# Prompt attention of a decoder step: split fp32r products against plain fp32 in halves of TensorE's array

## The chip, the cores and the metric

The kernel runs on one core of one Trainium2 chip. The metric is the device time of one execution in microseconds, the median of several. The engines are named as the profile names them: PE is TensorE (PEld its weight loads), DVE is VectorE, ACT is ScalarE, POOL is GpSimd, SP is SyncE, whose queue issues DMAs.

## The reference, cut to what matters

One layer of a decoder is computed for a prompt of 1024 tokens and for a sample group of 8 x 8 tokens. The change touches only the attention of the prompt. It has 8 heads of stick-breaking attention and 8 heads of dilated attention, all of width 64.

```python
def _sb_attend(q, k, v, mask, sb_bias):            # kind SB, strictly causal
    z = jnp.einsum('bqhd,bkhd->bhqk', q, k) * (q.shape[-1] ** -0.5) + sb_bias[...]
    log_1m = jnp.where(mask, jax.nn.log_sigmoid(-z), 0.0)
    excl = lax.cumsum(log_1m, axis=3, reverse=True) - log_1m
    a = jnp.where(mask, jnp.exp(jax.nn.log_sigmoid(z) + excl), 0.0)
    return jnp.einsum('bhqk,bkhd->bqhd', a, v)

def _dilated_prompt(q, k, v, rel_bias):            # kind DIL, three dilations, one softmax over all
    for window, dil in ((128, 1), (512, 4), (2048, 16)):
        ...
        logits = where(valid, q.k * scale + bias(distance), -inf)
        lse = logsumexp(logits); p = exp(logits - lse); o = p @ v
    return sum of the o's weighted by softmax of the lse's
```

The three dilations together are one softmax over all earlier keys, whose bias depends on the distance alone and holds the logarithm of how many dilations reach that key. The kernel computes it so, from a table `by_distance`.

## The kernel before, in words

The kernel is a row of stages, one after the other: transposing the tokens, the input projection, a stage that writes keys and values in their natural layout, the attention of the prompt (`prompt_stage`), the attention of the sample group, the output projection, the MLP, and the final norm. A stage ends with a barrier of all engines, so no work of one runs beside another's.

`prompt_stage` walks over four pairs of heads (`j`), and in each over 32 units: 16 of kind SB, then 16 of kind DIL. A unit `t` is one head and one tile of 128 queries against all keys up to it, so it is 128 to 1024 columns wide; the widths go up for the first head of the pair and down for the second. All five engines run the same walk, each a few steps later than the one before it, and wait for each other through counting semaphores:

- Step 0, TensorE `score`: queries times keys. To reach fp32 accuracy with the one-pass type fp32r, each operand is split into a rounded high part and the rest. `q_both` holds the high part of 64 rows and the low part in the other 64 rows, so one product with `k_hi` and one with `k_lo` give all four parts over 128 rows (line 958). For kind SB a bf16 product adds the causal mask (line 962). There are two score buffers of 1024 columns.
- Kind SB: ScalarE `gate` makes the sigmoids `take` and `stay` (lines 1035, 1037); VectorE `broken` makes the running product of `stay` from the right with a scan (line 1117) and multiplies it into `take` (line 1121).
- Kind DIL: VectorE `dilated` adds the bias (line 1134) and takes the maximum (1142) and its negative (1144); ScalarE `exponent` makes the exponentials with their sum (1043); VectorE `invert` inverts the sum (1149); ScalarE `soften` scales the weights by it (1048).
- Step 2, TensorE `turn`: transposes of the weights, in blocks of 128 columns, into one PSUM tile of 1024 columns (line 972). ScalarE `turned_hi` copies them out rounded (1054), and VectorE `turned_lo` writes the rest (1155). The next unit's transposes wait for line 1155.
- Step 3, TensorE `values`: 256 columns at a time (high and low weights) against high and low values as the 128 columns of the other operand (line 983). The two halves of the result are added: ScalarE copies the left half (1063), VectorE adds the right one (1165).
- Eight times in a pair and kind, `fold_heads` brings both heads' outputs to the right rows with two plain fp32 products against a constant matrix (line 992), and ScalarE copies them out (1069).

GpSimd splits queries, keys and values (lines 892 to 910) for each head and kind, while the units of the former head run, and issues the store of the outputs. SP's queue loads one head at a time, twice into both halves of the rows. What sets the order is this written walk: each engine's queue is in order.

Plain fp32 products stand elsewhere in the program: sums over rows with `ones` (line 486), and the scores and values of the sample stage (lines 1428 and 1499). In program order a unit of the sample stage has 16 products at line 1428, each on 32 columns of the array; the trace shows 32 records for them, two for each product. At line 1499 it has 32 products on 16 columns each, and 64 records.

Of the kernel before, what the change touches and what calls it, by code (L numbers as in the profile page):

```python
# [727 lines left out]
def prompt_stage(nc, cx, qkvT, oT, by_distance, sb_bias, neg_causal, ident, fold, v_nat):  # L728

# [18 lines left out]
    NU = 4 * QT  # L748
    HU = 2 * QT
    WS = 4  # L750


    FW = SEQ // 4
    fold_with = {**{1 + c: (DIL, c) for c in range(4)}, **{HU + 1 + c: (SB, c) for c in range(4)}}


    units = [(u // HU, (u % QT, QT - 1 - u % QT)[u // QT % 2], u // QT % 2) for u in range(NU)]
    with ExitStack() as st:
# [3 lines left out]
        q_raw, k_raw = sb("q_raw", [P, SEQ]), sb("k_raw", [P, SEQ])  # L762
        v_raw = sb("v_raw", [P, QT, HD])
        q_both = sb("q_both", [P, 2, SEQ], F32R)
        k_hi = sb("k_hi", [P, 2, SEQ], F32R)
        k_lo = sb("k_lo", [P, 2, SEQ], F32R)
        v_both = sb("v_both", [P, 2, QT, 2, HD], F32R)
        bias = sb("bias", [P, HEADS, SEQ])
        stay = sb("stay", [P, 2, SEQ])
        take = sb("take", [P, WS, SEQ])  # L770
        prod = sb("prod", [P, SEQ + 1])
        wtsT = sb("wtsT", [P, 2, QT, 2, P], F32R)
        o_sum = sb("o_sum", [P, 2, 2, SEQ])
        o_left = sb("o_left", [P, 2, P])
        o_T = sb("o_T", [P, SEQ])
        folds = sb("folds", [P, 2, P])
        top = sb("top", [P, 2, 2])
        den = sb("den", [P, HU])
        inv = sb("inv", [P, HU])
# [4 lines left out]
        s_ps = st.enter_context(nc.psum_tensor("pr_scores", [P, 2, 2 * 512], F32))  # L784
        t_ps = st.enter_context(nc.psum_tensor("pr_turned", [P, SEQ], F32))
# [5 lines left out]
        tables_in, tables_ready, bias_in = sem("tables_in"), sem("tables_ready"), sem("bias_in")  # L791
        q_loaded, v_loaded, k_loaded = sem("q_loaded"), sem("v_loaded"), sem("k_loaded")
        q_hi_done, q_done, k_hi_done, qk_ready = sem("q_hi_done"), sem("q_done"), sem("k_hi_done"), sem("qk_ready")
        v_hi_done, v_ready = sem("v_hi_done"), sem("v_ready")
        scored, sb_gates, sb_scanned, sb_weights = sem("scored"), sem("sb_gates"), sem("sb_scanned"), sem("sb_weights")
        logits, topped, lowered, exped, inverted, dil_weights = (sem("logits"), sem("topped"), sem("lowered"),
                                                                 sem("exped"), sem("inverted"), sem("dil_weights"))
        turned, hi_out, turned_out, o_done, o_summed = (sem("turned"), sem("hi_out"), sem("turned_out"), sem("o_done"),
                                                        sem("o_summed"))
        left_out, folded, oT_free, oT_stored = sem("left_out"), sem("folded"), sem("oT_free"), sem("oT_stored")  # L800

        def pipeline(eng, step, late):

            for s in range(NU):
                step(0, None, s)
            with eng.Fori(1, PAIRS) as j:
                for s in range(NU):
                    step(j, j - 1, s)
            for s in range(late):
                step(None, PAIRS - 1, s)  # L810

        def unit(j, prev, t):

            return (j, t) if t >= 0 else (prev, t + NU)

        def no_former(j):
            return isinstance(j, int) and j == 0

        def width(t):
            return (units[t][1] + 1) * P  # L820

        with nc.Block() as block:
            @block.sync
            def _(sp):
                def load(j, x):
                    kind, h = x // 2, x % 2
                    rows = [j * P + (g * W + h * HD) for g in (3 * kind, 3 * kind + 1)]
                    rows = rows if isinstance(j, int) else [sp.snap(a) for a in rows]
                    head = j * 2 + h if isinstance(j, int) else sp.snap(j * 2 + h)

                    sp.wait_ge(q_done, j * 4 + (x + 1))
                    for half in range(2):
                        sp.dma_start(q_raw[half * HD:(half + 1) * HD, :], qkvT[ds(rows[0], HD), 0:SEQ]).then_inc(q_loaded, 16)

                    sp.wait_ge(qk_ready, j * 4 + (x + 1))
                    for half in range(2):
                        sp.dma_start(k_raw[half * HD:(half + 1) * HD, :], qkvT[ds(rows[1], HD), 0:SEQ]).then_inc(k_loaded, 16)

                    sp.wait_ge(v_ready, j * 4 + (x + 1))
                    sp.dma_start(v_raw[:, :, :], v_nat[kind][0, 0].rearrange("(t p) h d -> p t h d", p=P)[  # L840
                        :, :, ds(head, 1), :].rearrange("p t o d -> p t (o d)")).then_inc(v_loaded, 16)

                for x in range(4):
                    load(0, x)
                    if x == 0:
                        sp.dma_start(zb[:, 0, :], bass.AP(
                            sb_bias.tensor, sb_bias.offset, [[0, P], [1, HEADS]])).then_inc(tables_in, 16)
                        sp.dma_start(maskf[:, :], neg_causal).then_inc(tables_in, 16)
                        sp.dma_start(folds[:, :, :], fold).then_inc(tables_in, 16)
                    if x == 1:  # L850
                        for h in range(HEADS):

                            first = by_distance.offset + h * LD + DIST0 - (SEQ - 1)
                            sp.dma_start(bias[:, h, :], bass.AP(by_distance.tensor, first,
                                                                [[1, P], [1, SEQ]])).then_inc(bias_in, 16)
                with sp.Fori(1, PAIRS) as j:
                    for x in range(4):
                        load(j, x)

            @block.gpsimd  # L860
            def _(pool):
                pool.sem_inc(q_done, 1)
                pool.sem_inc(v_ready, 1)
                pool.sem_inc(qk_ready, 1)
                pool.sem_inc(oT_free, 1)

                def split_first_v():

                    pool.wait_ge(v_loaded, 16)
                    pool.tensor_copy(v_both[:, 0, :, 0, :], v_raw[:, :, :]).then_inc(v_hi_done, 1)  # L870
                    pool.wait_ge(v_hi_done, 1)
                    pool.tensor_tensor(out=v_both[:, 0, :, 1, :], in0=v_raw[:, :, :],
                                       in1=v_both[:, 0, :, 0, :].bitcast(F32), op=ALU.subtract).then_inc(v_ready, 1)
                    pool.wait_ge(qk_ready, 2)
# [62 lines left out]
            def _(pe):  # L937
# [58 lines left out]
                def step(j, prev, s):  # L996
                    if j is not None:
                        score(j, s)
# [950 lines left out]
```

## Time and profile before

| | |
|---|---|
| time, median of 3 runs (lowest, highest) | 2310.68 us (2309.94, 2316.21) |
| the profiled execution's own time | 2313.0 us |
| its span, first to last instruction | 2311.1 us |
| mean granted TensorE clock over the span | 0.891 |
| PE busy | 1813.8 us (78%) |
| DVE busy | 1080.2 us (47%) |
| ACT busy | 631.1 us (27%) |
| POOL busy | 685.1 us (30%) |
| the stage of the prompt's attention | 403.5 to 870 us of the span |

Busy time is the union of an engine's instructions. It is an average over stages with different limits, so it has to be read stage by stage. The granted clock is a share of full speed: 1.00 is 2.4 GHz and 0.50 is 1.2 GHz, and a value between them is a mix of the two over a stretch. Matmul records overlap each other, because their printed ends include the way through the array; how fast they follow one another is read from several in a row.

### The profile page before, as it was taken

Reading aid. Unit: us, or ns where it says so; the run is one execution under the profiler, and the core shown is the slowest. Engines: PE = TensorE matmul, PEld = TensorE weight load, DVE = VectorE, ACT = ScalarE, POOL = GpSimd, SP = SyncE. Lnnn points to the kernel's source line nnn. Section 1 sums busy time; section 2 is a strip of 40 time slices with the busy share of each in tenths; the row PEclk is TensorE's granted clock in tenths of the full one; section 3 lists DMA queues with packets and bytes.
Section 4 is the critical chain, followed back from the end, with each engine's and each line's share of the span. In section 5 each row is a group of like instructions: output and inputs, shape, how many; then the busy total and the mean of one; then the engine's idle time right before and its main releaser. Section 6 shows DMA issues by size and latency. Waiting matters only on the chain. (4 is left out here: it accounts for less than half of the span.)

```text
span 2311.1 us, 37788 instructions
## 1 busy us (share of the span) xinstructions
PE 1813.8 (78%) x15810; PEld 1645.1 (71%) x15810; DVE 1080.2 (47%) x1229; ACT 631.1 (27%) x1068; POOL 685.1 (30%) x473
## 2 busy tenths in 40 slices
PE   4999995577666671565566639799999999999998
PEld 4999993456555550243334438789999999999997
DVE  5301112899897972876676445562222222122223
ACT  4100001476767670222032130131212112121122
POOL 2112101434343402566556631122112122121120
PEclk7999996787888885778887879899999999999999
DMA  6222218622222104999999970143433334333332
GB/s 210 76 85 103 85 48 317 167 55 55 56 56 65 45 10 135 411 419 423 421 421 420 406 300 1 37 164 109 146 127 127 139 114 144 128 127 131 122 109 104
DMA packets 129657, 382.35 MB, mean 165 GB/s; under 512 B 35416, under 2 KB 68824, under 8 KB 117464
## 3 DMA queue, kind: packets, MB, share of 16 engines
q0 software_dynamic: 41344, 256.13, 28.3%
q1 hardware_dynamic: 84840, 122.25, 16.5%
q10 hardware_dynamic: 3360, 2.47, 0.4%
q8 instruction: 70, 1.15, 0.2%
q14 instruction: 43, 0.35, 0.1%
HBM read 345.10 MB, written 102.57 MB: 194 GB/s over the span
## 5 line engine op out<-in xcount | busy, mean ns | idle before, releaser
L404 POOL TENSOR_TENSOR mlp_w_lo<-mlp_raw,mlp_w_hi 128x2048 fp32r<-128x2048 f32 x30 | 138.1, 4604 | 587.2 <-ACT mlp_w_hi L450 587.2
L1428 PE MATMUL sa_s<-sa_kT,sa_qd 128*32 128x256 f32 x1344 | 119.3, 516 | 156.7 <-DVE sa_kT L1692 96.3
L563 DVE TENSOR_TENSOR xT<-xT,mlp_acc 128x1088 f32<-128x1088 f32 x64 | 82.5, 1289 | 279.3 <-PE mlp_acc L145 279.3
L972 PE MATMUL pr_turned<-ident,pr_take 128*128 128x128 f32 x576 | 100.2, 307 | 139.7 <-DVE pr_wtsT L1155 126.2
L1428 PEld LDWEIGHTS sa_s<-sa_kT,sa_qd 128*32 128x32 f32 x1344 | 50.3, 141 | 209.1 <-DVE sa_kT L1692 103.5
L145 PE MATMUL mlp_acc<-n_hi,mlp_w_hi 128*128 128x272 f32 x1024 | 172.2, 290 | 20.6 <-POOL mlp_w_lo L121 16.3
L972 PEld LDWEIGHTS pr_turned<-ident,pr_take 128*128 128x128 f32 x576 | 69.5, 155 | 165.4 <-issue 165.3
L1692 DVE STREAM_TRANSPOSE sa_kT<-sa_k_in 128x2048 f32<-128x2048 f32 x64 | 147.2, 2307 | 81.8 <-DMA sa_k_in<-in_cache_sb_k,sa_k_rows 79.5
L145 PE MATMUL mlp_acc<-mlp_h_hi,mlp_w_hi 128*128 128x272 f32 x1024 | 170.6, 288 | 4.0 <-DVE mlp_h_lo L559 4.0
L145 PE MATMUL mlp_acc<-n_hi,mlp_w_lo 128*128 128x272 f32 x1024 | 171.1, 289 | 0.0
L145 PE MATMUL mlp_acc<-n_lo,mlp_w_hi 128*128 128x272 f32 x1024 | 171.1, 289 | 0.0
L145 PE MATMUL mlp_acc<-mlp_h_lo,mlp_w_hi 128*128 128x272 f32 x1024 | 169.8, 288 | 0.0
L145 PE MATMUL mlp_acc<-mlp_h_hi,mlp_w_lo 128*128 128x272 f32 x1024 | 169.8, 288 | 0.0
L145 PEld LDWEIGHTS mlp_acc<-n_hi,mlp_w_hi 128*128 128x128 f32 x1024 | 145.9, 190 | 21.6 <-POOL mlp_w_lo L121 16.5
L556 DVE SCALAR_TENSOR_TENSOR mlp_h<-mlp_acc,mlp_root 128x1088 f32<-128x1088 f32 x32 | 41.3, 1291 | 239.1 <-PE mlp_acc L145 238.7
L145 PEld LDWEIGHTS mlp_acc<-mlp_h_hi,mlp_w_hi 128*128 128x128 f32 x1024 | 143.9, 188 | 5.7 <-DVE mlp_h_lo L559 5.7
L145 PEld LDWEIGHTS mlp_acc<-n_lo,mlp_w_hi 128*128 128x128 f32 x1024 | 145.3, 189 | 0.0
L145 PEld LDWEIGHTS mlp_acc<-n_hi,mlp_w_lo 128*128 128x128 f32 x1024 | 145.3, 189 | 0.0
L145 PE MATMUL qkv_acc<-n_hi,qkv_w_hi 128*128 128x272 f32 x768 | 129.5, 291 | 18.4 <-POOL qkv_w_lo L121 14.0
L145 PEld LDWEIGHTS mlp_acc<-mlp_h_lo,mlp_w_hi 128*128 128x128 f32 x1024 | 144.0, 188 | 0.0
L145 PEld LDWEIGHTS mlp_acc<-mlp_h_hi,mlp_w_lo 128*128 128x128 f32 x1024 | 143.9, 188 | 0.0
L334 DVE TENSOR_TENSOR qkv_out<-qkv_acc,qkv_root 128x1088 f32<-128x1088 f32 x24 | 31.0, 1291 | 239.7 <-PE qkv_acc L145 239.3
(196 smaller groups left out, 3827.2 us busy)
## 6 DMA issues: line engine op xcount, KB each, us to landing
out<-in_cache_win_k POOLq DMA_DIRECT2D x16, 2040.0 KB, 8.6
out<-in_cache_win_v POOLq DMA_DIRECT2D x16, 2040.0 KB, 8.6
mlp_raw<-in_w_up SPq DMA_DIRECT2D x16, 1024.0 KB, 11.7
mlp_raw<-in_w_down SPq DMA_DIRECT2D x16, 1024.0 KB, 11.2
qkvT<-qkv_out SPq DMA_DIRECT2D x24, 544.0 KB, 2.7
qkv_raw<-in_w_in SPq DMA_DIRECT2D x12, 1024.0 KB, 5.5
na_rows_in<-qkvT SPq DMA_DIRECT2D x16, 544.0 KB, 6.7
out<-na_nat POOLq DMA_DIRECT2D x4, 2048.0 KB, 9.6
```

Source lines behind the costliest of these rows:

```text
L145: last = pe.matmul(out[:, b, 0:BW], w[:, k, w_cols], x[:, k, b * BW:(b + 1) * BW], start=(k == 0 and part == 0), stop=(k == kn - 1 and par ...
L334: dve.tensor_tensor(in_banks(out[:, q % 2, :]), acc[:, q % 2, :, 0:BW], in_banks(root[:, g, :]), ALU.mult).then_inc(acc_out, 1)
L404: pool.tensor_tensor(out=ring.lo[:, n % 2, :], in0=ring.raw[:, n % 2, :], in1=ring.hi[:, n % 2, :].bitcast(F32), op=ALU.subtract).then_inc ...
L556: dve.scalar_tensor_tensor(out=in_banks(act_h[:, c % 2, :]), in0=acc[:, c % 2, :, 0:BW], scalar=0.0, in1=in_banks(root[:, :]), op0=ALU.max ...
L563: dve.tensor_tensor(in_banks(xT[:, c, :]), in_banks(xT[:, c, :]), acc[:, c % 2, :, 0:BW], ALU.add).then_inc(added, 1)
L972: last = pe.transpose(t_ps[:, a:a + P], take[:, t % WS, a:a + P], ident[:, :])
L1428: last_one = pe.matmul(out[h * 32:(h + 1) * 32, :], qd[:, k, x, :], keys[:, x, :], start=(b == 0), stop=(b == 1 and stop))
L1692: dve.transpose(kT[:, n % 2, :, q * P:(q + 1) * P].rearrange("p x (j k) -> p j x k", k=32), k_in[:, x % KS, :, :].rearrange("p j (x d) -> ...
```

## The change

`prompt_stage` is written anew. All products are plain fp32, and nothing is split into high and low parts. A unit is now one tile of queries of both heads of a pair, so there are 64 units (`NU`), 8 of kind SB and 8 of kind DIL in each pair, with narrow and wide ones in turn (`order`: 0, 7, 1, 6, 2, 5, 3, 4). Scores are made in pieces of at most 512 columns, for head 0 in the upper 64 rows of the array and for head 1 in the lower 64 rows, each into its own PSUM bank. The outputs of the heads come from the left and the right 64 columns of the array and land in the upper and lower 64 partitions of one tile, so nothing has to be folded. In kind DIL the weights stay unscaled: a second series of products against `ones` makes the sums of the weights in the same layout as the output, VectorE inverts that tile of 128x128 and multiplies. Turned weights go through two PSUM buffers of 512 columns, one head and piece at a time, and ScalarE alone copies them out. GpSimd only reverses the queries of kind DIL, once a pair. SP's queue loads two heads at a time, for two pairs ahead, and stores the outputs. The four walks over pairs are now written out without a loop.

The core of the diff:

```diff
-    NU = 4 * QT
-    HU = 2 * QT
+    NU = 2 * PAIRS * QT
     WS = 4
+    PW = 512
+    order = [q for i in range(QT // 2) for q in (i, QT - 1 - i)]
...
+        s_ps = st.enter_context(nc.psum_tensor("pr_scores", [P, 2, 2, PW], F32))
+        t_ps = st.enter_context(nc.psum_tensor("pr_turned", [P, 2, PW], F32))
...
             def _(sp):
+                def load(j, k):
...
+                        sp.wait_ge(scored, pieces_to(past))
+                        sp.wait_ge(o_done, past)
...
+                for j in range(PAIRS):
+                    for k in range(2):
+                        past = kind_units(j, k)[1]
+                        if j + 2 < PAIRS:
+                            load(j + 2, k)
+                        sp.wait_ge(o_copied, past)
+                        row = j * P + k * W
+                        sp.dma_start(oT[row:row + P, 0:SEQ], o_T[:, k, :]).then_inc(stored[k], 16)
...
+                def score(s):
...
+                    for p, (a, n) in enumerate(pieces(s)):
+                        g = piece[s, p]
+                        if g >= 2:
+                            k2, count = scores_read[g - 2]
+                            pe.wait_ge((gates, logits)[k2], count)
+                        masked = k == SB and a + n == width(s)
+                        for h in range(2):
+                            rows, cols = slice(h * HD, (h + 1) * HD), slice(q * P, (q + 1) * P)
+                            queries = q_back[rows, j % 2, cols] if k == DIL else q_in[rows, SB, j % 2, cols]
+                            last = pe.matmul(s_ps[:, g % 2, h, 0:n], queries, k_in[rows, k, j % 2, a:a + n], start=True,
+                                             stop=not masked)
...
+                def turn(s):
...
+                        for h in range(2):
+                            g = turned_piece[s, p, h]
+                            if g >= 2:
+                                pe.wait_ge(copied, g - 1)
+                            for b in range(0, n, P):
+                                last = pe.transpose(t_ps[:, g % 2, b:b + P], take[:, s % WS, h, a + b:a + b + P], ident[:, :])
...
+                def values(s):
...
+                    for c in range(q + 1):
+                        for h in range(2):
+                            last = pe.matmul(o_ps[h * HD:(h + 1) * HD, s % 2, 0:P], v_in[:, k, j % 2, c, h * HD:(h + 1) * HD],
+                                             wtsT[:, s % 2, h, c, :], start=(c == 0), stop=(c == q))
+                    if k == DIL:
+                        for c in range(q + 1):
+                            for h in range(2):
+                                last = pe.matmul(o_ps[h * HD:(h + 1) * HD, s % 2, P:2 * P], ones[:, 0:HD],
+                                                 wtsT[:, s % 2, h, c, :], start=(c == 0), stop=(c == q))
...
+                def gate(s):
...
+                    if w >= 2:
+                        act.wait_ge(sb_weights, w - 1)
...
+                for s in range(NU + 3):
+                    if s < NU and kind(s) == SB:
+                        gate(s)
+                    if 0 <= s - 2 < NU:
+                        copy_out(s - 2)
+                    if s < NU and kind(s) == DIL:
+                        exponent(s)
...
-                def turned_lo(j, t):
-
-                    dve.wait_ge(hi_out, j * NU + (t + 1))
...
+                def o_out(s):
...
+                    if k == SB:
+                        dve.tensor_copy(out, o).then_inc(o_copied, 1)
+                        return
...
+                    dve.reciprocal(one_over[:, :], o_ps[:, s % 2, P:2 * P]).then_inc(inverted, 1)
+                    dve.wait_ge(inverted, r + 1)
+                    dve.tensor_tensor(out, o[:, ::-1], one_over[:, ::-1], ALU.mult).then_inc(o_copied, 1)
```

On TensorE, in the middle of the stick-breaking units of the first pair, a step of before is the scores of one head and tile (`pr_scores`), the transposes of the unit two steps back (`pr_turned`) and the values of the unit three steps back (`pr_o`):

```order
L958 MATMUL pr_scores<-pr_k_hi,pr_q_both 128x512 [waits pr_sb_gates]
L958 MATMUL pr_scores<-pr_k_lo,pr_q_both 128x512
L958 MATMUL pr_scores<-pr_k_hi,pr_q_both 128x512
L958 MATMUL pr_scores<-pr_k_lo,pr_q_both 128x512
L962 MATMUL pr_scores<-pr_maskb,pr_identb 128x128
L972 MATMUL pr_turned<-ident,pr_take 128x128 [waits pr_sb_weights,pr_turned_out]
L972 MATMUL pr_turned<-ident,pr_take 128x128 x5
L983 MATMUL pr_o<-pr_wtsT,pr_v_both 128x256 [waits pr_o_summed,pr_turned_out]
L983 MATMUL pr_o<-pr_wtsT,pr_v_both 128x256 x4
```

The changed kernel at the same place, from the masks of a wide unit to the first scores of the next one:

```order
L883 MATMUL pr_scores<-pr_maskb,pr_identb 128x128 x2
L895 MATMUL pr_turned<-ident,pr_take 128x128 [waits pr_copied,pr_sb_weights]
L895 MATMUL pr_turned<-ident,pr_take 128x128 x3
L895 MATMUL pr_turned<-ident,pr_take 128x128 [waits pr_copied]
L895 MATMUL pr_turned<-ident,pr_take 128x128 x3
L895 MATMUL pr_turned<-ident,pr_take 128x128 [waits pr_copied]
L895 MATMUL pr_turned<-ident,pr_take 128x128
L895 MATMUL pr_turned<-ident,pr_take 128x128 [waits pr_copied]
L895 MATMUL pr_turned<-ident,pr_take 128x128
L907 MATMUL pr_o<-pr_wtsT,pr_v_in 64x128 [waits pr_o_copied,pr_copied]
L907 MATMUL pr_o<-pr_wtsT,pr_v_in 64x128 x5
L879 MATMUL pr_scores<-pr_k_in,pr_q_back 128x128 [waits pr_gates,pr_q_turned,pr_qk_loaded10]
```

One wait for the whole of `turn` became a wait for each of four pieces, for ScalarE's copy of two pieces back, and the values and the next scores stand behind them.

On VectorE, in the dilated units of the first pair, a step of before has six instructions:

```order
L1149 RECIPROCAL pr_inv<-pr_den 128x1 [waits pr_exped]
L1134 SCALAR_TENSOR_TENSOR pr_take<-pr_scores,pr_bias 128x768 [waits pr_scored,pr_turned]
L1142 TENSOR_REDUCE pr_top<-pr_take 128x1 [waits pr_exped,pr_logits]
L1144 TENSOR_SCALAR pr_top<-pr_top 128x1 [waits pr_topped]
L1155 TENSOR_TENSOR pr_wtsT<-pr_turned,pr_wtsT 128x4x128 [waits pr_hi_out]
L1165 TENSOR_TENSOR pr_o_sum<-pr_o_left,pr_o 128x128 [waits pr_left_out]
```

The changed kernel, for a unit of both heads:

```order
L1008 SCALAR_TENSOR_TENSOR pr_take<-pr_scores,pr_bias 128x2x512 [waits pr_scored,pr_turned]
L1008 SCALAR_TENSOR_TENSOR pr_take<-pr_scores,pr_bias 128x2x256 [waits pr_scored]
L1014 TENSOR_REDUCE pr_top<-pr_take 128x2 [waits pr_dil_weights,pr_logits]
L1028 RECIPROCAL pr_one_over<-pr_o 128x128 [waits pr_o_copied,pr_o_done]
L1030 TENSOR_TENSOR pr_o_T<-pr_o,pr_one_over 128x128 [waits pr_inverted]
```

The two instructions on turned weights and half outputs are gone; a reciprocal of 128 columns and a product stand at the end of the step.

## Rows read from the trace of the kernel before

**Rows 1.** Stretches: us, then busy us (x instructions) of each engine, clock, DMA share, GB/s.

```profile
403.50:870.00 466.50, 307.06 (x1728) 256.16 (x1728) 403.25 (x648) 305.90 (x616) 159.03 (x100) 0.83 0.24 64
```

**Rows 2.** Waits from 410 to 870 us: who, for whom, us in total, times, longest.

```profile
PE pr_turned L972 <- DVE pr_wtsT L1155: 126.2, 99, 4.1
...
ACT pr_take L1035 <- DVE pr_take L1121: 30.5, 23, 3.2
```

**Rows 3.** By line, VectorE, 410 to 870 us: busy us, mean ns, idle before.

```profile
L1117 DVE TENSOR_TENSOR_SCAN pr_prod<-pr_stay 128x128 f32<-128x128 f32 (+7 forms) x64 | 102.3, 1598 | 3.2 <-ACT pr_stay L1037 3.1
...
L1155 DVE TENSOR_TENSOR pr_wtsT<-pr_turned,pr_wtsT 128x128 fp32r<-128x128 f32 (+7 forms) x128 | 96.4, 753 | 13.8 <-ACT pr_wtsT L1054 12.4
...
L1121 DVE TENSOR_TENSOR pr_take<-pr_take,pr_prod 128x128 f32<-128x128 f32 (+7 forms) x64 | 72.2, 1129 | 2.2
...
L1134 DVE SCALAR_TENSOR_TENSOR pr_take<-pr_scores,pr_bias 128x128 f32<-128x128 f32 (+7 forms) x64 | 48.4, 756 | 8.2 <-issue 4.2 <-PE pr_scores L958 2.4 <-PE pr_turned L972 1.0
...
L1165 DVE TENSOR_TENSOR pr_o_sum<-pr_o_left,pr_o 128x128 f32<-128x128 f32 x128 | 35.3, 277 | 2.9 <-ACT pr_o_left L1063 2.3 <-issue 0.6
```

**Rows 4.** By line, ScalarE, 410 to 870 us.

```profile
L1054 ACT ACTIVATE pr_wtsT<-pr_turned 128x128 fp32r<-128x128 f32 (+7 forms) x128 | 82.5, 645 | 32.6 <-PE pr_turned L972 32.3
...
L1048 ACT ACTIVATE pr_take<-pr_take,pr_inv 128x128 f32<-128x128 f32 (+7 forms) x64 | 49.7, 777 | 17.8 <-DVE pr_inv L1149 17.8
L1043 ACT ACTIVATE pr_take<-pr_take,pr_top 128x128 f32<-128x128 f32 (+7 forms) x64 | 49.6, 775 | 24.8 <-DVE pr_top L1144 24.5
...
L1035 ACT ACTIVATE pr_take<-pr_scores,pr_zb 128x128 f32<-128x128 f32 (+7 forms) x64 | 47.5, 742 | 59.6 <-DVE pr_take L1121 30.5 <-PE pr_scores L962 24.6 <-PE pr_turned L972 4.4
...
L1063 ACT ACTIVATE pr_o_left<-pr_o 128x128 f32<-128x128 f32 x128 | 35.3, 276 | 0.6 <-PE pr_o L983 0.6
```

**Rows 5.** Timeline, VectorE and ScalarE, 640 to 662 us: start, us, instruction.

```profile
659.12 2.28 DVE L1117 TENSOR_TENSOR_SCAN pr_prod<-pr_stay 128x1024 f32<-128x1024 f32 x1
661.44 1.22 DVE L1121 TENSOR_TENSOR pr_take<-pr_take,pr_prod 128x1024 f32<-128x1024 f32 x1
...
643.57 0.68 ACT L1037 ACTIVATE pr_stay<-pr_scores,pr_zb 128x512 f32<-128x512 f32 x1
...
649.98 0.60 ACT L1054 ACTIVATE pr_wtsT<-pr_turned 128x512 fp32r<-128x512 f32 x1
...
655.76 1.11 ACT L1037 ACTIVATE pr_stay<-pr_scores,pr_zb 128x1024 f32<-128x1024 f32 x1
656.76 0.81 ACT L1054 ACTIVATE pr_wtsT<-pr_turned 128x768 fp32r<-128x768 f32 x1
```

**Rows 6.** Timeline, TensorE, 640 to 662 us.

```profile
648.31 0.63 PE L972 MATMUL pr_turned<-ident,pr_take 128*128 128x128 f32 x4
...
659.16 0.96 PE L972 MATMUL pr_turned<-ident,pr_take 128*128 128x128 f32 x7 [0.82 <-DVE pr_wtsT L1155]
```

**Rows 7.** Plain fp32 products elsewhere: timeline, TensorE, then the same stretches' clock.

```profile
1522.94 1.99 PE L486 MATMUL mlp_acc<-mlp_root,ones 128*128 128x272 f32 x8
...
1202.28 3.30 PE L1428 MATMUL sa_s<-sa_kT,sa_qd 128*32 128x256 f32 x32 [3.81 <-DVE sa_kT L1692]
1205.52 0.92 PE L1493 MATMUL sa_w<-ident,sa_logit 128*128 128x128 f32 x4
1206.36 1.83 PE L1499 MATMUL sa_o<-sa_v_in,sa_wtsT 128*16 128x128 f32 x60
...
1202.20:1205.60 3.40, 3.32 (x33) 1.46 (x34) 2.16 (x5) 0.00 (x0) 2.49 (x3) 0.57 1.02 426
1206.30:1208.30 2.00, 2.00 (x67) 1.73 (x66) 0.92 (x1) 1.45 (x5) 1.39 (x3) 1.00 1.00 410
1522.80:1525.00 2.20, 2.13 (x11) 1.47 (x9) 0.00 (x0) 0.03 (x1) 0.00 (x0) 1.00 0.58 183
```

**Rows 8.** Timeline, VectorE, MLP stage: a reciprocal.

```profile
1526.17 6.95 DVE L549 RECIPROCAL mlp_root<-mlp_root 128x1088 f32<-128x1088 f32 x1 [3.69 <-ACT mlp_root L436]
```

**Rows 9.** Timeline, the stage's first product.

```profile
414.55 0.58 PE L958 MATMUL pr_scores<-pr_k_hi,pr_q_both 128*128 128x256 f32 x1 [22.13 <-DVE pr_zb L1106]
```

More of the change, by code:

```diff
@@ L802, in pipeline @@
[L802 to L820, printed above, removed]
+        tables_in, tables_ready = sem("tables_in"), sem("tables_ready")
@@ L822, in prompt_stage, with kind_units @@
+        turned, copied, o_done, o_copied = sem("turned"), sem("copied"), sem("o_done"), sem("o_copied")
+        stored = [sem(f"stored{k}") for k in range(2)]
+        def kind_units(j, k):
+            return j * 2 * QT + k * QT, j * 2 * QT + (k + 1) * QT
         with nc.Block() as block:
@@ L824, in _ @@
             def _(sp):
[L825 to L855, printed above, removed]
@@ L990, in fold_heads @@
-                def fold_heads(bank, kind, c):
-                    for h in range(2):
-                        last = pe.matmul(o_ps[:, bank, 2 * P:2 * P + FW], folds[:, h, :], o_sum[:, kind, h, c * FW:(c + 1) * FW],
-                                         start=(h == 0), stop=(h == 1))
-                    return last
-                def step(j, prev, s):
-                    if j is not None:
-                        score(j, s)
-                    for late, do in ((2, turn), (3, values)):
-                        ju, t = unit(j, prev, s - late)
-                        if ju is not None and not (j is None and t < NU - late):
-                            do(ju, t)
@@ new lines, in turn @@
+                def turn(s):
+                    j, k, q = unit(s)
+                    pe.wait_ge((sb_weights, dil_weights)[k], (1, 2)[k] * (of_kind(s, k) + 1))
+                    for p, (a, n) in enumerate(pieces(s)):
+                        for h in range(2):
+                            g = turned_piece[s, p, h]
[3 more added lines that the diff above has]
+                                last = pe.transpose(t_ps[:, g % 2, b:b + P], take[:, s % WS, h, a + b:a + b + P], ident[:, :])
+                            last.then_inc(turned, 1)
@@ L1013, in _ @@
+                for s in range(NU + 3):
+                    if s < NU:
+                        score(s)
+                    if 0 <= s - 2 < NU:
+                        turn(s - 2)
+                    if 0 <= s - 3 < NU:
+                        values(s - 3)
             @block.scalar
@@ L1184, in sample_stage @@
+                for s in range(NU + 4):
+                    if s < NU and kind(s) == DIL:
+                        dilated(s)
+                    if 0 <= s - 1 < NU and kind(s - 1) == SB:
+                        broken(s - 1)
+                    if 0 <= s - 4 < NU:
+                        o_out(s - 4)
 def sample_stage(nc, cx, qkvT, oT, by_distance, sb_bias, page_table, sb_caches, win_caches, new_v, neg_new, neg_other,
```

428 lines of the change are left out of this document (155 added, 273 removed).

## The prediction

> **What bounds the kernel now.** I first cut the run into stages with the view of busy time by stretch. The stage that the change rewrites runs from 403.5 to 870 us, 466 us of a span of 2311.1 [rows 1]; nothing outside it is edited, so the whole answer is what these 466 us become. In it VectorE is busy 403 us, TensorE 307, ScalarE 306, GpSimd 159, and the mean granted TensorE clock is 0.83 [rows 1]. The view of waits says who waits: TensorE stands 126.2 us before its transposes for VectorE's write of the low halves of the turned weights (line 1155), and ScalarE 30.5 us before its sigmoids for VectorE's product (line 1121) [rows 2]. So VectorE's queue sets the pace. The view by line shows what fills it: the scan 102.3, low halves 96.4, product 72.2, logits 48.4 (the maximum over as many columns, not shown) and the sum of two half outputs 35.3 us [rows 3]. ScalarE has 82.5 us of copies, 49.7 of scaling by the inverted sum, 49.6 of exponentials, 47.5 of sigmoids to `take` (the sigmoids to `stay`, as many and of the same shapes, not shown) and 35.3 of left half outputs [rows 4].
>
> **What goes and stays on VectorE.** Lines 1155 (96.4) and 1165 (35.3) go [rows 3]: 132 us. The scans keep their columns. In each kind, four pairs of two heads with 36 blocks of 128 columns make 36,864 columns. A quiet scan of 1024 columns takes 2.28 us, that is 2.2 ns a column, and a quiet product 1.22 us [rows 5]; the totals of 102.3 and 72.2 are above this, since GpSimd's splitting works on the same memory then, and it goes too. In place: a copy of 128x128 for each of 32 stick-breaking units and, for each of 32 dilated ones, a reciprocal of 128 columns and a product. Line 549 takes 6.95 us for 1088 columns [rows 8], so about 0.95 for 128 with the fixed part; the small operations go by line 1165's 277 ns [rows 3]. I count units by twos, one narrow (on average 2.5 blocks) and one wide (6.5 blocks), each now holding both heads. VectorE then has for two stick-breaking units 5.6 (wide scans and product) + 2.4 + 0.5 = 8.5 us. For two dilated ones logits and maximum go by the product's 1.05 ns a column and 0.15 fixed, 3.9 + 1.7, and the outputs 2 x 1.23: 8.1 us.
>
> **ScalarE.** Scaling (49.7) and left halves (35.3) go [rows 4]. The quiet sigmoid takes 1.11 us for 1024 columns and 0.68 for 512, so 0.84 ns a column and 0.26 fixed, and the next starts 0.1 before the printed end [rows 5]. Two stick-breaking units need 12 sigmoids with 4608 columns and 6 copies with 2304 (a 512-column copy 0.60, fixed 0.16): 5.8 + 2.3 = 8.1 us. Two dilated units: 4 exponentials and the copies, about 5.5 us.
>
> **TensorE.** A bound from both sides is needed here, since this stage has no plain fp32 product of this shape. The sums with ones in the MLP stage are plain fp32: four products make 8 records in 1.99 us, 272 columns each, at clock 1.00 [rows 7]: 0.229 us a record (0.84 ns a column), two records a product. The sample stage has the column tiles: 16 products of 256 columns make 32 records in 3.30 us at clock 0.57, that is 8 rounds of four at once; 15 rounds of 128 columns take 1.83 us at clock 1.00, 0.11 a round [rows 7]. So tiles of columns run beside each other in plain fp32, and their loads hide. No row shows tiles of rows, which the scores use (64 rows a head). If they pair up as well, two units' scores take 1152 columns x 1.68 ns = 1.9 us; one after the other 3.9. I take 1.9 because the nearest rows, tiles of the same array, pair. Transposes: seven take 0.96 and four 0.63, so 0.11 each [rows 6], 18 of them 2.0. Values: 9 steps of two rounds, 2.0 us; one by one 3.9. The sums with ones repeat the values' rounds in dilated units, 2.0 more (3.9). Masks, 128 columns like a transpose, 4 x 0.11 = 0.45.
>
> Each unit now goes from half rows to the full array, to half columns and back. In the sample stage the full-array transposes start 0.06 us before the end of the tiled scores, and the tiled values 0.08 before the end of the transposes [rows 7], where equal ones overlap 0.16 us (four 0.27 ones in 0.63): about 0.1 us a change, 0.6 for two units. Sums: stick-breaking 6.9, dilated 8.4 us at full clock.
>
> The Trainium skill has a rule against this change: TensorEngine Tiling (Array Packing), section Key Properties, says that going from one tiling mode to another drains TensorE. The 0.1 us just read agrees with it in kind; a drain of a whole record (0.2 us) would add 0.6 us to two units, 19 us in all. A second one, TensorE: Matmul & The Clock Gate, Part 3, has weight loads hide beside running products only where the row group differs; by it the loads of the column halves stand bare and the values cost what they cost one by one. The 0.11 us rounds above, in one row group, speak against it.
>
> **The loop of stick-breaking units.** In order, TensorE does scores(s), turn(s-2), values(s-3); ScalarE gate(s), copies(s-2). From a wide gate's start: gate 4.1; TensorE has turned two of four pieces and waits, since there are two buffers; copies 1.0, then two more beside the late transposes, 0.9, with values of a narrow unit starting at 5.6; values 0.65 and narrow scores with mask 0.95, so the next gate starts at 7.2 (ScalarE idle 1.2). That gate takes 1.75 and its copies 0.7; TensorE meanwhile turns 0.65, does wide values 1.4 and the first score piece 1.25: 10.5. VectorE's loop through the two `stay` slots, wide gate 4.1 + 5.6, is below. With 5.2 us of TensorE in the cycle at a clock of 0.85 (stage now 0.83 [rows 1]) it is 11.5. Sixteen times: 184 us.
>
> **Dilated units.** TensorE 8.4 / 0.85 = 9.9, and 0.7 for the third and fourth piece waiting for a copy: 10.6, above VectorE's 8.1. Sixteen times: 169 us. What is late next is TensorE, no longer VectorE.
>
> **Sum.** Start as now, 11 us from the stage's start at 403.5 [rows 1] to the first score [rows 9] (the splitting on VectorE goes, but the tables now queue behind 1.5 MB; -3 to +4). Filling 6, seven changes of kind 12 (a late wide product behind the first logits, a table load of 1.3), the tail 6. 11 + 6 + 184 + 169 + 12 + 6 = 388, against 466: 78 us less. The profiled execution took 2313.0 us for its span of 2311.1, 2.3 above the median of 2310.7, so I predict 2310.7 - 78 = 2233 us.
>
> GpSimd's splitting, its `oT` store and the fold products go; I count them at nothing, as VectorE and ScalarE cover them. Loads and stores move to SP's queue: SP waits at each pair for `o_copied`, and behind it stand only loads for two pairs later, a pair being some 88 us; so nothing is late.
>
> **Rivals.**
> (a) The two score products do not pair: the two row halves take turns. For: no row shows them. Against: column tiles pair. Stick-breaking + 1.6 us for two (narrow 0.53 and first wide piece 0.85, at the clock), dilated + 2.3: 210 + 206 + 35 = 451, 15 less than now: 2296. By the skill's TensorE page, Part 3, four row tiles gave 3.07 times, so a pairing of about three quarters; an estimate from that is a third of the way to this case.
> (b) Slower: no halves pair, so plain fp32 costs four passes of the whole array. Values add 2.3 to two stick-breaking units, values and sums 4.6 to two dilated ones, on top of (a): 15.4 and 17.5, 246 + 280 + 35 = 561: 2406. It decides from an average of 13.5 us for two units ((466 - 35) / 32), against my 11.0. Against it stand the rounds of 0.11 us; for it, that those tiles are 16 and 32 columns wide, not 64.
> (c) Better: a denser TensorE is granted 0.95 and bubbles are half of what I drew. Stick-breaking 10.5, dilated 9.2, 168 + 147 + 35 = 350: 2195. For: in the run of plain products the clock was 1.00 [rows 7]; against: waits and transposes remain.
> (d) The halves are not what decides but a chain I missed at the kind changes or in the ring: up to 40 us anywhere.
>
> **Chances.** Forecast (2215 to 2260) 0.58, (a) 0.17, (b) 0.09, (c) 0.13, (d) 0.03. The range holds the forecast, (c) and (a): 2185 to 2310. Faster by over 0.3% (7 us, about what a measurement can tell): 0.86; within: 0.05, the edge of (a); slower: 0.09.
>
> **What would show it.** The stage between its first load and the oT stores 388 us long (350 to 451); score records of the two heads starting within some 10 ns of each other, value records likewise, every 0.11 us at full clock; VectorE under 270 us busy, no wait of TensorE for VectorE among the longest, but TensorE waiting for ScalarE's copies in the transposes, and ScalarE for scores; VectorE's reciprocal near 0.95 us. I am wrong if score records of 512 columns follow at 0.43 us head after head (a), or TensorE is busy for over 400 us of the stage (b).

## The result and the profile after

The changed kernel takes 2213.5 us (median of four runs, 2211.8 to 2215.5) beside 2313.1 us (2309.9 to 2316.2) for the kernel before on the same chip: a ratio of 0.957, 95% interval 0.955 to 0.959. It is about 100 us faster; 78 were forecast. The 2310.7 us ahead of the prediction were the median of three runs of the kernel before; with a fourth run it is 2313.1. The forecast was 2233 us, 2215 to 2260; 2213.5 lies just under that, towards rival (c), 2195, and inside the whole range of 2185 to 2310.

The page of the profile after, busy time by engine:

```profile
span 2210.0 us, 37863 instructions
PE 1801.2 (81%) x16830; PEld 1590.4 (72%) x16834; DVE 936.0 (42%) x857; ACT 556.4 (25%) x908; POOL 531.8 (24%) x377
```

VectorE is down by 144 us, GpSimd by 153, ScalarE by 75, and TensorE by only 13. The span falls by 101.

Busy time by stretch, with the columns of [rows 1]: the whole stage; then its seven stretches, cut where the first score of a kind starts (SB, DIL and so on; the eighth, the last dilated one, runs into the tail).

```profile
400.20:769.70 369.50, 294.39 (x2752) 205.36 (x2752) 259.00 (x276) 231.35 (x456) 5.14 (x4) 0.90 0.17 58
...
408.80:458.00 49.20, 35.74 (x204) 20.55 (x204) 28.81 (x25) 32.21 (x67) 3.06 (x2) 0.67 0.49 171
458.00:495.30 37.30, 34.08 (x351) 24.18 (x349) 30.96 (x34) 22.12 (x40) 0.00 (x0) 0.99 0.17 58
495.30:544.00 48.70, 35.98 (x344) 25.35 (x342) 33.59 (x35) 35.65 (x75) 1.04 (x1) 0.93 0.13 44
544.00:581.10 37.10, 35.20 (x350) 25.23 (x348) 30.94 (x34) 22.19 (x40) 0.00 (x0) 0.95 0.17 58
581.10:632.10 51.00, 38.46 (x342) 26.79 (x340) 33.51 (x35) 35.75 (x75) 1.04 (x1) 0.87 0.13 42
632.10:669.40 37.30, 34.09 (x350) 24.17 (x348) 30.96 (x34) 22.11 (x40) 0.00 (x0) 0.99 0.04 16
669.40:718.10 48.70, 35.97 (x343) 25.34 (x341) 33.27 (x35) 35.66 (x75) 0.00 (x0) 0.93 0.03 12
```

The stage takes 369.5 us against 466.5 [rows 1], 97 less. In a dilated stretch TensorE is busy 34 to 35 of 37 us at a clock of 0.95 to 0.99: it paces them. In a stick-breaking one nobody is busy all the time: TensorE 36, ScalarE 36, VectorE 34 of 49. The stage begins 3.3 us earlier than before (400.2 against 403.5). That need not be the change's: in the runs below, whose code ahead of the stage is the same, the stage begins anywhere between 399.5 and 403.3 us, and its first product between 407.9 and 412.2.

The waits from 405 to 780 us (who, for whom, us in total, times, longest) answer to [rows 2]:

```profile
PE pr_turned L895 <- ACT pr_wtsT L963: 53.1, 39, 3.4
DVE pr_prod L990 <- ACT pr_stay L943: 52.1, 24, 4.5
ACT pr_wtsT L963 <- PE pr_turned L895: 51.4, 46, 3.1
DVE pr_take L1008 <- PE pr_scores L879: 37.5, 20, 5.4
ACT pr_take L953 <- DVE pr_top L1014: 18.1, 20, 2.2
```

TensorE's 126 us for VectorE are gone. It now waits 53 us for ScalarE's copies, and VectorE waits for the other two.

By line, 405 to 775 us, columns as in [rows 3]: VectorE and ScalarE answer to [rows 3, 4], TensorE to [rows 6, 7]:

```profile
L907 PE MATMUL pr_o<-pr_wtsT,pr_v_in 128*64 128x128 f32 x1152 | 84.0, 294 | 2.5 <-DVE pr_o_T L1023 2.5
L990 DVE TENSOR_TENSOR_SCAN pr_prod<-pr_stay 128x128 f32<-128x128 f32 (+7 forms) x64 | 83.9, 1352 | 52.2 <-ACT pr_stay L943 52.1
...
L879 PE MATMUL pr_scores<-pr_k_in,pr_q_in 64*128 64x512 f32 (+3 forms) x192 | 48.7, 616 | 20.9 <-DVE pr_zb L980 19.7 <-ACT pr_stay L943 1.2
...
L994 DVE TENSOR_TENSOR pr_take<-pr_take,pr_prod 128x256 f32<-128x256 f32 (+7 forms) x32 | 44.1, 1378 | 1.1
...
L912 PE MATMUL pr_o<-pr_wtsT,ones 128*64 128x128 f32 x576 | 38.5, 280 | 0.0
L1028 DVE RECIPROCAL pr_one_over<-pr_o 128x128 f32<-128x128 f32 x32 | 30.4, 950 | 6.1 <-PE pr_o L912 5.7
```

The lines of 96.4 and 35.3 us [rows 3] are gone. The scan and the product have the same columns as before, yet fell from 102.3 to 83.9 and from 72.2 to 44.1: GpSimd no longer works beside them (159 us of the stage before, 5 now); the last section has the rows for this reading. The reciprocal, which had no row before, takes 0.950 us.

TensorE in the timeline (start, us, instruction), first in a dilated stretch, then in a stick-breaking one from a wide unit to the next:

```profile
562.52 1.97 PE L907 MATMUL pr_o<-pr_wtsT,pr_v_in 128*64 128x128 f32 x32
564.32 1.92 PE L912 MATMUL pr_o<-pr_wtsT,ones 128*64 128x128 f32 x32
566.16 1.56 PE L879 MATMUL pr_scores<-pr_k_in,pr_q_back 64*128 64x512 f32 x8
567.65 1.09 PE L895 MATMUL pr_turned<-ident,pr_take 128*128 128x128 f32 x8
...
515.62 1.04 PE L895 MATMUL pr_turned<-ident,pr_take 128*128 128x128 f32 x8
519.89 1.61 PE L895 MATMUL pr_turned<-ident,pr_take 128*128 128x128 f32 x8 [3.23 <-ACT pr_wtsT L963]
521.44 0.70 PE L907 MATMUL pr_o<-pr_wtsT,pr_v_in 128*64 128x128 f32 x4
522.06 1.65 PE L879 MATMUL pr_scores<-pr_k_in,pr_q_in 64*128 64x384 f32 x4
```

Thirty-two records of values follow in 1.80 us (564.32 - 562.52), 16 rounds of 0.11: the column halves run two by two. The scores of both heads, eight records with 3072 columns, take 1.49 us to the transposes; at 0.84 ns a column one after the other they would take 2.6. In the individual records the two heads start 6 to 7 ns apart, values every 0.109 us. In the second part TensorE turns two pieces, stands 3.23 us for the copy, and then turns eight blocks in 1.61 us instead of 1.04: 0.4 us after it comes back the granted clock falls from 1.00 to 0.50 (1.2 GHz), and it stays there from 520.3 to 523.7 us. ScalarE's rows in the same place show the copy that it waited for, behind the gate of the wide unit:

```profile
515.04 0.69 ACT L941 ACTIVATE pr_take<-pr_scores,pr_zb 128x512 f32<-128x512 f32 x1 [1.72 <-PE pr_scores L879]
...
519.19 1.14 ACT L963 ACTIVATE pr_wtsT<-pr_turned 128x512 f32<-128x512 f32 x2
...
527.48 0.69 ACT L941 ACTIVATE pr_take<-pr_scores,pr_zb 128x512 f32<-128x512 f32 x1 [0.87 <-PE pr_scores L879]
```

The next wide gate starts 12.4 us after the first one. The clock of that cycle, in two parts:

```profile
515.00:519.60 4.60, 1.66 (x14) 0.93 (x10) 1.88 (x4) 4.56 (x9) 0.77 (x1) 1.00 0.89 299
519.60:527.50 7.90, 7.61 (x62) 4.87 (x62) 7.69 (x6) 4.49 (x11) 0.27 (x1) 0.78 0.23 87
```

### The profile page after: what moved, and what is told of

Same layout as the page of the kernel before. It is cut to its first block and busy times, and to the rows that moved or that the text cites. A ratio compares the mean times of both kernels' runs of the same rounds, so it can differ in the third digit from the quotient of the medians.

```text
span 2210.0 us, 37863 instructions
## 1 busy us (share of the span) xinstructions
PE 1801.2 (81%) x16830; PEld 1590.4 (72%) x16834; DVE 936.0 (42%) x857; ACT 556.4 (25%) x908; POOL 531.8 (24%) x377
## 5 line engine op out<-in xcount | busy, mean ns | idle before, releaser
L1285 PE MATMUL sa_s<-sa_kT,sa_qd 128*32 128x256 f32 x1344 | 129.0, 550 | 155.6 <-DVE sa_kT L1549 97.1
L895 PE MATMUL pr_turned<-ident,pr_take 128*128 128x128 f32 x576 | 96.1, 303 | 58.4 <-ACT pr_wtsT L963 53.1
L1237 POOL DMA_INDIRECT sa_v_in<-in_cache_sb_v,sa_v_rows x128 | 124.3, 971 | 50.1 <-issue 38.8
```

Source lines behind the costliest of these rows:

```text
L895: last = pe.transpose(t_ps[:, g % 2, b:b + P], take[:, s % WS, h, a + b:a + b + P], ident[:, :])
L1237: pool.indirect_dma_start(v_in[:, n % VS, a, :], None, src, bass.IndirectOffsetOnAxis(ap=rows, axis=0)).then_inc(v_loaded[n % VS], 16)
L1285: last_one = pe.matmul(out[h * 32:(h + 1) * 32, :], qd[:, k, x, :], keys[:, x, :], start=(b == 0), stop=(b == 1 and stop))
```

## The experiments

Each was timed in three rounds beside the kernel before: 2309.4 us beside the runs on the new way of dividing and on the stick-breaking units, 2310.9 beside the others. Compared below is the time with the changed kernel's 2213.5 us, beside which the kernel before had 2313.1, so differences of 2 to 4 us say nothing. The theory was the prediction's: both kinds of halves pair, TensorE paces the dilated units, and the copies behind the gate hold the stick-breaking ones. The rivals say where else the gain could come from.

**Do column halves pair, and does the order matter?** Values and sums head by head instead of in turn.

```diff
-                    for c in range(q + 1):
-                        for h in range(2):
+                    for h in range(2):
+                        for c in range(q + 1):
```

> The same products as the changed kernel; only the order of values and sums is by head (all of the left 64 columns, then all of the right ones) and no longer in turn. If halves pair only with neighbours in TensorE's queue, nine steps of two rounds become eighteen for two units: 2.0 us more for two stick-breaking units and 4.0 for two dilated ones at full clock, 16 times each, about 100 us: 2310 us, no gain left over the kernel before; value records then follow each other every 0.11 us. Rival: each half has its own queue and order does not matter: 2213 us and pairs of records 6 ns apart.

2259.1 us (2257.2 to 2261.7), ratio to before 0.978 (0.976 to 0.979): 46 us slower than the changed kernel, between the two expectations. Its stretches, and its values:

```profile
504.70:562.50 57.80, 45.25 (x344) 33.90 (x342) 34.07 (x34) 35.45 (x74) 2.28 (x1) 0.86 0.12 37
562.50:605.00 42.50, 40.70 (x349) 30.88 (x348) 31.17 (x35) 22.38 (x41) 0.00 (x0) 0.99 0.14 51
...
L907 PE MATMUL pr_o<-pr_wtsT,pr_v_in 128*64 128x128 f32 x1152 | 123.7, 291 | 1.0 <-DVE pr_o_T L1023 1.0
L912 PE MATMUL pr_o<-pr_wtsT,ones 128*64 128x128 f32 x576 | 60.1, 284 | 0.0
...
564.33 2.45 PE L907 MATMUL pr_o<-pr_wtsT,pr_v_in 128*64 128x128 f32 x24
```

These 24 records take 2.39 us to the next work. In turn, 12 rounds of 0.11 would take 1.3; one by one, 24 of 0.109 would take 2.6. The individual records say why. A record doesn't name its half, but the starts fall into two series of twelve: the first head's, every 0.109 us from 564.334 on, and the other half's, whose first starts at 565.264, when three of the first head's are still to come. From there the two run beside each other. Where the second head's values give way to the first head's sums, the line numbers show the same: the first record of the sums (L912) starts ahead of three records of the values (L907).

```profile
508.12 0.32 PE L912 MATMUL pr_o<-pr_wtsT,ones 128*64 128x128 f32 x1
...
508.44 0.27 PE L907 MATMUL pr_o<-pr_wtsT,pr_v_in 128*64 128x128 f32 x1
```

So neighbours in the queue pair, and a few records further on, but not twelve. Column pairing is shown, and that the order of the loop decides how much of it is had. Since some pairs are left, 46 us are less than the whole of it.

**Do row halves pair?** Both heads' scores from the upper 64 rows; the second head's own scores are left out.

```diff
-                            rows, cols = slice(h * HD, (h + 1) * HD), slice(q * P, (q + 1) * P)
+                            rows, cols = slice(0, HD), slice(q * P, (q + 1) * P)
```

> Both heads' scores are made from the upper 64 rows (so head 1 gets head 0's scores; this leaves head 1's own scores out), with the same shapes and counts. The two products can then not run beside each other. Mine: 0.53 us (narrow) and 0.85 (first wide piece) on the path of two stick-breaking units and 1.9 for two dilated ones, at the clock: 23 + 32 = 55 us more, 2268 us, which is what pairing of row halves is worth. Rival: the scores are hidden behind ScalarE and VectorE: at most 2225 us.

2290.4 us (2288.3 to 2293.4), ratio 0.992 (0.990 to 0.994): 77 slower. Stretches, scores by line, and eight of their records:

```profile
577.50:622.60 45.10, 43.65 (x351) 30.05 (x349) 31.54 (x35) 22.67 (x41) 0.00 (x0) 0.94 0.14 48
622.60:683.50 60.90, 50.52 (x342) 34.12 (x340) 33.26 (x34) 35.38 (x74) 1.04 (x1) 0.82 0.11 35
...
L879 PE MATMUL pr_scores<-pr_k_in,pr_q_in 64*128 64x512 f32 (+3 forms) x192 | 91.1, 618 | 19.7 <-DVE pr_zb L980 19.7
...
551.41 3.03 PE L879 MATMUL pr_scores<-pr_k_in,pr_q_in 64*128 64x512 f32 x8
```

Row halves pair in the changed kernel: its 48.7 us for the same 192 records become 91.1. Eight records that took 1.49 us to the next work there take 2.96 here, and at full clock those of 512 columns follow at 0.43 us, one at a time. Dilated stretches are 7.7 us longer, 1.9 for two units, close to the 2.0 that the scores' sizes give. Stick-breaking ones are about 12 longer, 3 for two units, twice what was expected. Their clock is 0.77 to 0.82 where it was 0.87 to 0.93. This is the prediction's rival (a) made true, at 2290 us where (a) said 2296.

**What is the new way of dividing worth?** The sum with the exponentials, a reciprocal of two columns and ScalarE's scaling come back; sums with ones and the division of outputs go.

```diff
-                                last = pe.matmul(o_ps[h * HD:(h + 1) * HD, s % 2, P:2 * P], ones[:, 0:HD],
...
+                        act.activation(x, x, ACT.Exp, bias=top[:, r % 2, h:h + 1], scale=-1.0,
+                                       accum_out=den[:, r % 2, h:h + 1]).then_inc(exped, 1)
...
+                        act.activation(x, x, ACT.Copy, scale=inv[:, r % 2, h:h + 1]).then_inc(dil_weights, 1)
```

> The second half of the change undone inside the new form: ScalarE's exponentials give their sums, VectorE inverts 128x2 numbers, ScalarE scales the weights before the transposes; no products against ones, no division of outputs. TensorE loses 2.0 us and VectorE 2 for two dilated units, ScalarE gains about 3.5 (from 5.5 to 9). Mine: ScalarE is then as late as TensorE is now and the time stays at 2205 to 2225 us. Rival: the sums by TensorE are simply a cost of 2.0 us and undoing them saves 30 us: 2183. Other rival: the longer chain exponential, reciprocal, scaling, copy stops ScalarE before each unit: 2240.

2225.5 us (2223.8 to 2229.3), ratio 0.963 (0.961 to 0.966): 12 slower (15 by the ratios; the stage of the profiled execution is 385.9 us long instead of 369.5, 16 more). So of the 100 us the new way of dividing gives 12 to 16, and the rest of the change 84 to 88. How this rest is split between VectorE's dropped work, GpSimd's, and units of two heads, no run shows. A dilated stretch, and two waits:

```profile
457.96:499.10 41.14, 30.09 (x268) 19.42 (x266) 28.25 (x38) 32.42 (x68) 0.00 (x0) 0.99 0.15 52
...
DVE pr_inv L1034 <- ACT pr_take L949: 45.2, 24, 2.2
PE pr_turned L896 <- ACT pr_wtsT L966: 78.5, 43, 4.4
```

TensorE is 4 us less busy than with the sums, ScalarE 10 busier, and the stretch 3.8 longer. The scaling stands in a chain (exponentials, VectorE, ScalarE, transposes); the sums fill TensorE's own queue and wait for nobody. The expectation had 2205 to 2225 us, with ScalarE as late as TensorE; the time is at its edge, but ScalarE is busy for only 32.4 of 41.1 us, so by these waits it is the chain of its other rival that costs, if not as much as its 2240 us.

**What paces the dilated units?** A copy in place of the reciprocal (outputs are then not divided by the sums); and no sums at all (the reciprocal reads the outputs instead).

```diff
-                    dve.reciprocal(one_over[:, :], o_ps[:, s % 2, P:2 * P]).then_inc(inverted, 1)
+                    dve.tensor_copy(one_over[:, :], o_ps[:, s % 2, P:2 * P]).then_inc(inverted, 1)
```

> A plain copy stands in place of the reciprocal of 128 columns (so the outputs of dilated units are not divided): 0.28 for 0.95 us on VectorE, 32 times, 21 us of its busy time. Mine: TensorE sets the pace of dilated units, VectorE waits for scores there, so it goes down by 5 us at most, to 2208 or more. Rival: VectorE (31 of 37.3 us busy in each dilated stretch) sets it: 2192 us.

2210.9 us (2209.9 to 2212.9), ratio 0.957 (0.955 to 0.959): no difference.

```diff
-                    if k == DIL:
-                        for c in range(q + 1):
-                            for h in range(2):
-                                last = pe.matmul(o_ps[h * HD:(h + 1) * HD, s % 2, P:2 * P], ones[:, 0:HD],
-                                                 wtsT[:, s % 2, h, c, :], start=(c == 0), stop=(c == q))
...
```

> The products against ones are left out (the reciprocal is taken of the output's own tile, so the sums of the weights are missing); VectorE does what it did. TensorE has 2.0 us less for two dilated units. Mine: it sets the pace, so they go from 9.3 us to about 8.0, where VectorE's 8.1 holds them: 20 us less, 2193 us. Rival: VectorE or ScalarE set the pace: 2210 to 2213 us.

2192.2 us (2186.8 to 2193.1), ratio 0.948 (0.946 to 0.950): 21 faster. The first dilated stretch without the reciprocal, then without the sums:

```profile
458.20:495.50 37.30, 34.11 (x352) 24.21 (x350) 28.78 (x35) 22.13 (x40) 0.00 (x0) 0.99 0.17 58
```

```profile
458.80:491.50 32.70, 29.45 (x266) 19.57 (x264) 29.82 (x33) 21.41 (x39) 0.00 (x0) 0.99 0.20 66
```

Two us off VectorE leave the stretch at 37.3; 4.6 us off TensorE make it 32.7, 4.6 less, where VectorE (29.8) is close behind. TensorE paces these units, as forecast, and its work can shrink by at least 1.1 us for two units before another engine does.

**What holds the stick-breaking units?** Two edits shorten TensorE's standstill for the copies. In the first, ScalarE copies out a piece after each piece of its gate. In the second, TensorE does the values between the first and the second piece of the transposes.

```diff
                         last.then_inc(gates, 1)
+                        if s >= 2:
+                            copy_piece(s - 2, p)
...
```

> ScalarE copies the turned weights piece by piece between the pieces of the sigmoids in stick-breaking units, and no longer after all of them; dilated units are untouched. Mine: TensorE no longer stands about 3 us at the third piece of a wide unit, and ScalarE's stop of about 2 us after its copies goes to about 1: from 12.2 to 11.2 us for two units, 16 less, 2197 us. Rival: VectorE's loop through the stay slots takes over, since the wide sigmoids now end 1.0 us later (4.1 + 1.0 + 5.6 + waits = 10.9) and the time stays at 2210.

2194.6 us (2189.7 to 2197.5), ratio 0.950 (0.947 to 0.953): 19 faster.

```diff
...
-                        turn(s - 2)
+                        turn(s - 2, 0)
                     if 0 <= s - 3 < NU:
                         values(s - 3)
+                    if 0 <= s - 2 < NU:
+                        turn(s - 2, 1)
```

> TensorE does the values of the unit three back between the two pieces of a wide unit's transposes, where it waited for ScalarE's copies. Mine: 0.65 us less for two stick-breaking units and 0.7 for two dilated ones: 21 less, 2192 us. Rival: what TensorE gains there it waits for scores' buffers afterwards: 2210 or more.

2196.4 us (2191.6 to 2204.6), ratio 0.952 (0.948 to 0.956): 17 faster. In the profiled executions TensorE's wait for the copies falls from 53 us to 31 in the first and to 34 in the second, and a stick-breaking stretch from 48.7 to 45.1 and 44.9. The second was also to shorten the dilated units, by 0.7 us for two; their stretches stay at 37.0 to 37.1, so the whole gain is in the stick-breaking ones. And both together:

> Both orders together, all results kept. Mine: 11.0 us for two stick-breaking units and 8.7 for two dilated ones: 19 + 10 = 29 less than the changed kernel, 2184 us. Rival: they hide the same wait, so no more than the better of the two alone.

2182.2 us (2181.8 to 2183.4), ratio 0.945 (0.943 to 0.947): the fastest of all that compute the whole reference, 31 us under the changed kernel and 127 under the kernel before beside it. A stick-breaking and a dilated stretch of it, and waits of the stage:

```profile
489.10:532.50 43.40, 35.89 (x341) 24.95 (x340) 34.44 (x35) 34.52 (x74) 1.04 (x1) 0.92 0.15 49
532.50:567.90 35.40, 32.87 (x351) 23.92 (x350) 30.22 (x35) 21.70 (x43) 0.00 (x0) 1.00 0.17 61
...
ACT pr_wtsT L970 <- PE pr_turned L898: 44.9, 38, 2.7
DVE pr_prod L998 <- ACT pr_stay L948: 38.6, 16, 4.4
ACT pr_take L946 <- DVE pr_take L1002: 31.6, 11, 5.1
...
PE pr_turned L898 <- ACT pr_wtsT L970: 18.5, 20, 1.3
```

The wait of TensorE for the copies fell from 53.1 to 18.5 us, and the same work takes 43.4 us instead of 48.7. The dilated stretch takes 35.4 us, which neither edit did alone; why isn't known. By the waits, late next is the loop through the two `stay` slots, which no run tests: ScalarE's gate for VectorE's product, VectorE's scan for the gate, up to 5.1 us at a time.

## Why the prediction was right, and where it wasn't

- **The size**: 100 us were gained and 78 forecast. The working of the prediction ends 19 us above the stage's 369.5; the dilated units are 20 too long in it, by one term, and the rest nearly cancels.
- **What bounds the stage** was read from [rows 1 to 4]: VectorE. With its low halves and half sums gone it is 259 us busy where under 270 were expected, and no wait of TensorE for it is among the longest, but for 19.7 us at the stage's start. The outcome fits this reading; no run took VectorE's work alone away.
- **The price of plain fp32 in halves**, the largest unknown, held: rounds of 0.11 us for values and sums as in [rows 7], and row halves in pairs, for which no row stood. The two experiments on pairing show what hung on it, 46 and 77 us. A kernel with no pairing at all, rival (b), wasn't run. If the two losses add up (an estimate), 46 + 77 = 123 us are more than the 100 gained, and the sign of the result rests on both kinds of pairs.
- **A change of shape** was put at 0.1 us. From the last transpose to the first value record, and from there to the scores, 0.20 us lie between starts where equal ones lie 0.11 apart: 0.1 it is. By the rule of the Trainium skill, TensorEngine Tiling (Array Packing), Key Properties, TensorE drains there. The trace agrees in kind, at 0.1 us and not the 0.2 that the prediction gave as an estimate. The other rule of the Trainium skill, TensorE: Matmul & The Clock Gate, Part 3, that loads overlap running products only where the row group differs (the same part also lets a load into the background weight buffer go ahead), is not borne out as the prediction told it: 32 loads in one row group ran within 16 rounds of 0.11 us.
- **The dilated units** are the mis-sized term: 169 us forecast, 148.6 measured in four stretches (37.3 + 37.1 + 37.3 + 36.9; the last is cut at 755 us, near where a next kind would begin). The step that failed is "8.4 / 0.85": the clock of the old stage, 0.83 [rows 1], was carried to a queue that has hardly a gap. It was granted 0.95 to 0.99, and the 0.95 has its 0.50 at the start, from 544.2 to 547.6 us, behind the last standstill of the stick-breaking units; from there on the stretch has 1.00. With 0.97 the same working gives 8.4 / 0.97 + 0.7 = 9.4 us for two units, and 9.3 were measured. The "for" of rival (c), that dense plain products had 1.00 [rows 7], should have been read for these units alone.
- **The stick-breaking units**: 184 + 12 for changes of kind + 6 for filling = 202 forecast, 197.6 measured for the four stretches. The sum came close, and its parts less so. In the three later stretches a cycle from one wide gate to the next takes 12.4 to 12.5 us with a wide unit of seven blocks and 10.9, 12.4 and 10.9 with one of six, 11.9 on average where 11.5 was written for the size between. In the cycle shown, gate (4.1) and standstill came as drawn; the eight late transposes (five is the average) take 1.6 us and the values, scores and masks behind them 2.3, all but the first 0.4 at the clock of 0.50, and so the narrow gate starts 9.0 us after the wide one and not 7.2. The changes of kind and the filling cost less than the 18 us written: sixteen cycles of 11.9 are 190, which leaves some 7 (an estimate). They don't hide in the standstill: 3.45 us of it, the longest, come right after a change, and the last dilated unit but one has its values and sums behind it.
- **Start and tail**: 8.6 us from the stage's start to the first product (11 forecast), and 14.7 from 755 to 769.7 (6 forecast), where the last units have no other work beside their chains. All terms: 8.6 + 197.6 + 148.6 + 14.7 = 369.5, against 388.
- **After the stage** nothing changed (1440.3 against 1441.0 us), and the store on SP's queue was late for nobody.

## What to carry to other kernels

When two heads of 64 fit the array side by side, in rows or in columns, issue them in turn, record by record: losing most of the pairs in columns cost 46 us here, losing those in rows 77, and in plain fp32 both worked, which made splitting operands needless. Price a stage's new queue at the clock that queues as dense as it are granted, stage by stage, and expect a lower one after most standstills: of 16 of 2.8 to 3.5 us in this stage, 14 find TensorE at 0.50 within 2 us of their end, and the two from 528.9 to 531.9 and from 703.0 to 706.0 us have none. Before taking a standstill as given, ask what the waiting engine has ready a few lines further down: two edits that only change the order were worth 31 us.

## What was not expected of the hardware

- TensorE starts a product for the free half of the array ahead of about three waiting records for the busy half: 565.264 us against 565.367, 565.476 and 565.585 in the run with values head by head. Beyond that it keeps the order, which cost 46 us.
- With scores in one half TensorE was busy more and yet had a lower clock in the stick-breaking stretches (0.82 at 50.5 of 60.9 us busy, against 0.87 at 38.5 of 51.0), and the loss there was 3 us for two units and not 1.5. That the clock is the reason, and which of TensorE's pauses it answers to, isn't settled.
- VectorE's scans of the same 36,864 columns went from 102.3 to 83.9 us, and the products from 72.2 to 44.1, of which only 5 (32 instructions fewer at 0.15) come from their number. A pair of 1024-column scans takes 4.47 us in the changed kernel, 2.24 each, as the quiet one of before [rows 5]. The trace of before shows what slowed the others. Of its eight 1024-column scans, the six with GpSimd idle for over 90% of their time took 2.28 us each, and the two beside its splitting, for a third and for nearly all of their time, 3.24 and 3.38; of the products of 1024 columns, four took 1.22 to 1.23 us and the four beside it 1.88 to 1.95. Summed over all widths, scans and products beside GpSimd took about 16 and 24 us more than quiet ones, nearly all of what went. Not everything on VectorE was slowed: the logits (line 1134, which read PSUM) and the maximum took the same time beside GpSimd as alone. No run took GpSimd's work alone away, so what this was worth of the 100 us stays open.

```profile
505.61 4.47 DVE L990 TENSOR_TENSOR_SCAN pr_prod<-pr_stay 128x1024 f32<-128x1024 f32 x2 [4.53 <-ACT pr_stay L943]
```

One of the slow scans of before, and what GpSimd did beside it:

```profile
439.97 3.38 DVE L1117 TENSOR_TENSOR_SCAN pr_prod<-pr_stay 128x1024 f32<-128x1024 f32 x1
...
441.40 2.78 POOL L899 CAST pr_k_hi<-pr_k_raw 128x1024 fp32r<-128x1024 f32 x1 [0.20 <-POOL pr_q_both L895]
```
